# Head scores in three split products, sigmoids without reciprocals, and gate tile, rotation and root rows at other points, in a three-layer block kernel

## What is computed

```python
r = jax.nn.sigmoid(einsum(xb, wa) + ba)
i = jax.nn.sigmoid(einsum(xb, wx) + bx)
log_a = (LRU_C * r) * jax.nn.log_sigmoid(lam)
a = jnp.exp(log_a)
b = jnp.sqrt(-jnp.expm1(2.0 * log_a)) * (i * xc)      # h_t = a_t h_(t-1) + b_t
```

## Time and profile before

| | |
|---|---|
| median of 3 runs | 3032.59 us |
| the profiled execution's own time | 3033.25 us |
| its span, first to last instruction | 3031.2 us |
| TensorE busy (matmul) | 2968.0 us, 98% |
| VectorE, ScalarE, GpSimd busy | 53%, 43%, 45% |
| TensorE waiting for other work, all waits over 0.1 us | about 53 us |

### The profile page before, as it was taken

One profiled execution on the slowest core, in us unless ns is written; L12 is line 12 of the kernel. 1 busy time (PEld: TensorE's weight loads), 2 busy tenths in 40 slices (PEclk: granted clock), 3 DMA queues, 4 the chain that ended last, 5 costly groups with the idle time before them and its releaser, 6 DMA issues. The chain is left out here.

```text
span 3031.2 us, 48608 instructions
## 1 busy us (share of the span) xinstructions
PE 2968.0 (98%) x17338; PEld 2407.8 (79%) x17338; DVE 1616.7 (53%) x2411; ACT 1304.1 (43%) x2552; POOL 1351.8 (45%) x1022
## 2 busy tenths in 40 slices
PE   8999999999999999999999999999999999999998
PEld 6888888877777788878888877788888888777886
DVE  5377666655657306653556575551435565755412
ACT  6545444354556334453333334453533333344532
POOL 4444444443433356454444433344644444433444
PEclk9999999999999999999999999999999999999999
DMA  6322222222222334333322222243343222222433
GB/s 240 107 86 108 83 83 82 72 84 83 81 77 78 131 119 153 104 118 136 118 91 87 91 84 70 77 147 102 121 149 118 91 86 92 84 70 74 149 101 107
DMA packets 79010, 313.30 MB, mean 103 GB/s; under 512 B 7440, under 2 KB 11920, under 8 KB 51472
## 3 DMA queue, kind: packets, MB, share of 16 engines
q1 hardware_dynamic: 54832, 266.62, 26.1%
q10 hardware_dynamic: 24032, 44.76, 4.2%
HBM read 293.01 MB, written 18.35 MB: 103 GB/s over the span
## 5 line engine op out<-in xcount | busy, mean ns | idle before, releaser
L340 POOL TENSOR_TENSOR w_low<-w_raw,w_high 128x512 fp32r<-128x512 f32 x844 | 1136.1, 1351 | 1525.2 <-ACT w_high L851 1502.5
L405 PE MATMUL z<-u_high,w_high 128*128 128x512 f32 x3216 | 1277.4, 397 | 15.3 <-DVE work L1491 14.6
L406 PE MATMUL z<-u_low,w_high 128*128 128x512 f32 x3216 | 1257.9, 391 | 0.0
L851 ACT ACTIVATE w_high<-w_raw 128x512 fp32r<-128x512 f32 x832 | 520.0, 629 | 1112.6 <-PE z L409 1075.9
L409 PE MATMUL z<-u_high,w_low 128*128 128x512 f32 x3216 | 862.3, 390 | 0.0
L405 PEld LDWEIGHTS z<-u_high,w_high 128*128 128x128 f32 x3216 | 605.8, 188 | 165.2 <-issue 32.4
L409 PEld LDWEIGHTS z<-u_high,w_low 128*128 128x128 f32 x3216 | 605.0, 188 | 127.7
L406 PEld LDWEIGHTS z<-u_low,w_high 128*128 128x128 f32 x3216 | 606.3, 189 | 119.7
L1867 DVE TENSOR_TENSOR work<-work 128x512 f32<-128x512 f32 x78 | 90.9, 1165 | 277.5 <-ACT work L1140 264.8
L1491 DVE TENSOR_TENSOR work<-z,work 128x512 f32<-128x512 f32 x110 | 76.1, 692 | 181.9 <-PE z L409 145.3
L363 POOL TENSOR_TENSOR pass_weights<-w_raw,pass_weights 128x512 fp32r<-128x512 f32 x96 | 134.4, 1424 | 62.3 <-ACT pass_weights L1053 61.8
(11 more groups left out here) (341 smaller groups left out, 3698.3 us busy)
## 6 DMA issues: line engine op xcount, KB each, us to landing
w_raw<-in_wt SPq DMA_DIRECT2D x213, 1024.0 KB, 4.9
w_raw<-in_wt SPq DMA_DIRECT2D x144, 256.0 KB, 3.0
out_hT<-work ACTq DMA_DIRECT2D x10, 1024.0 KB, 5.8
work<-out_hT ACTq DMA_DIRECT2D x8, 1024.0 KB, 10.3
work<-in_xT SPq DMA_DIRECT2D x4, 1024.0 KB, 16.5
e_scratch<-work ACTq DMA_DIRECT2D x1, 4096.0 KB, 16.7
work<-in_xT ACTq DMA_DIRECT2D x4, 1024.0 KB, 10.9
mixed<-e_scratch ACTq DMA_DIRECT2D x4, 1024.0 KB, 9.2
```

The source lines that it names most:

```text
L340: pool.tensor_tensor(WL[:, 4 * q:4 * q + 4, :], RAW[:, t.odd, 512 * q:512 * q + 512].rearrange("p (k c) -> p k c", k=4), WH[:, 4 * q:4 * q ...
L405: pe.matmul(bank[:], WH[:, k, :], UH[:, k, :], start=(k == 0), stop=False)
L406: pe.matmul(bank[:], WH[:, k, :], UL[:, k, :], start=False, stop=False)
L851: act.activation(WH[:, 4 * q:4 * q + 4, :], RAW[:, n.odd, 512 * q:512 * q + 512].rearrange("p (k c) -> p k c", k=4), ACT.Copy).then_inc(se ...
```

## The change

The two heads' scores are formed from high and low parts of type fp32r, three products for each head, the heads taken in turn; `take_heads` makes the high parts by copies and the low parts by two more subtractions, on VectorE (`dif_scores` is changed as `att_scores` is, with its width w). The LRU's sigmoids are formed by exponential, logarithm, exponential on ScalarE; VectorE first reads both gates from PSUM, adds the bias and clips. The root row and the turn back stand one piece later, in the gated product's second half three pieces later. In the differential stages the first rotation is at point 7 in place of 6. In the first of them the gate tile is read at point 11 in place of 15, and the tile behind it right after the stage in place of point 3 of the next.

```diff
@@ -187 @@
+        QKH = nc.alloc_sbuf_tensor_at("heads_high", [P, 2, S], F32R, offset=work_at + 22 * S * 4)
+        QKL = sb("heads_low", [P, 2, S], F32R)
@@ -573 tensor engine, scores @@
+            def head_scores(n, hd, a, w):
+
+                o = slice(64 * hd, 64 * hd + 64)
+                q, k = ((QKH, QKH), (QKH, QKL), (QKL, QKH))[n]
+                return pe.matmul(SC[hd][:, 0:w], q[o, 0, a * P:(a + 1) * P], k[o, 1, 0:w], start=(n == 0), stop=(n == 2))
+
             def att_scores(j, a):
 
-                for hd in range(2):
-                    u = 2 * a + hd
-                    pe.wait_ge(sem("sm_done"), PRIMED + j * 8 + max(u - 1, 0))
-                    o = 64 * hd
-                    pe.matmul(SC[hd][:], row(QT)[o:o + 64, a * P:(a + 1) * P], row(KTR)[o:o + 64, :],
-                              start=True, stop=True).then_inc(sem("s_done"), 1)
+                for n in range(3):
+                    for hd in range(2):
+                        if n == 0:
+                            pe.wait_ge(sem("sm_done"), PRIMED + j * 8 + max(2 * a + hd - 1, 0))
+                        mm = head_scores(n, hd, a, S)
+                        if n == 2:
+                            mm.then_inc(sem("s_done"), 1)
...
@@ -770 tensor engine, norm_points @@
                 if pg:
-                    return {6: lambda: root_row(n),
-                            7: lambda: turn_back(n, (sem("pg_prod"), 14 + 2 * h), h, (0, 12), BACK_PG[h])}
-                return {3: lambda: root_row(n),
-                        4: lambda: turn_back(n, (sem("z_free"), t - T_HGG + (5 if h else 2)), h, (12,), BACK)}
+                    return {7 + 2 * h: lambda: root_row(n),
+                            8 + 2 * h: lambda: turn_back(n, (sem("pg_prod"), 14 + 2 * h), h, (0, 12), BACK_PG[h])}
+                return {4: lambda: root_row(n),
+                        5: lambda: turn_back(n, (sem("z_free"), t - T_HGG + (5 if h else 2)), h, (12,), BACK)}
@@ -947 ScalarE, ret_work @@
                 if p == 9:
-                    if cl is not None:
-                        act.wait_ge(sem("cl_ready"), cl)
+                    act.wait_ge(sem("gate_read"), PRIMED + j * 2 + 2)
                     for g in range(2):
-                        act.wait_ge(sem("gate_done"), j * 2 + g + 1)
-                        act.wait_ge(sem("scan_done"), PRIMED + j)
-                        act.activation(row(LR + g), SC[g][:], ACT.Exp, bias=SM[:, 32 + 6 * g + b:33 + 6 * g + b],
-                                       scale=-1.0).then_inc(sem("gate_read"), 1)
+                        sigmoid(LR + g, "r_ready")
                 if p == 10:
-                    act.wait_ge(sem("r_ready"), j + 1)
+                    act.drain()
@@ -1529 VectorE, take_heads @@
                 v.drain()
-                v.tensor_copy(row(QT), row(QN))
-                v.tensor_copy(row(KTR), row(KN)).then_inc(sem(done), 1)
+                for n, x in ((0, QN), (1, KN)):
+                    v.tensor_copy(QKH[:, n, :], row(x))
+                v.drain()
+                for n, x in ((0, QN), (1, KN)):
+                    i = v.tensor_tensor(QKL[:, n, :], row(x), QKH[:, n, :].bitcast(F32), ALU.subtract)
+                i.then_inc(sem(done), 1)
@@ -1688 VectorE, lru_work @@
                 if p == 9:
 
-                    v.wait_ge(sem("gate_read"), PRIMED + j * 2 + 2)
-                    v.tensor_scalar(view(LR, 0, [[1, 2 * S]]), view(LR, 0, [[1, 2 * S]]), 1.0, None, ALU.add)
-                    v.drain()
-                    v.reciprocal(R_, R_).then_inc(sem("r_ready"), 1)
-                    v.reciprocal(I_, I_)
+                    for g in range(2):
+                        v.wait_ge(sem("gate_done"), j * 2 + g + 1)
+                        v.tensor_scalar(row(LR + g), SC[g][:], SM[:, 32 + 6 * g + b:33 + 6 * g + b], GATE_MIN, ALU.subtract, ALU.max
+                                        ).then_inc(sem("gate_read"), 1)
                 if p == 10:
+                    v.wait_ge(sem("r_ready"), j * 2 + 2)
@@ -1789 VectorE, step @@
+                    if p == gate_taken_at:
+                        rstd_mul(t.plus(gate_tile_at), row(RW))
+                        bounded()
                     if work is not None:
...
-                            gate_tile(t.plus(gate_tile_at), gate[0], MIX[:, gate[1], :])
+                            if gate_taken_at is None:
+                                rstd_mul(t.plus(gate_tile_at), row(RW))
+                                bounded()
+                            gate_product(gate[0], MIX[:, gate[1], :])
@@ -2160 VectorE, the layer's order @@
-                dif = dict(rot=(CTD, STD, 32), scales=scd, take="dqt_ready", ends=(6, 10), gate_tile_at=2)
+                dif = dict(rot=(CTD, STD, 32), scales=scd, take="dqt_ready", ends=(7, 10), gate_tile_at=2)
                 step(Tile(T_L2 + R_DIF, (PER_LAYER, l)), gate=(gl + 6, 6), work="ret", j=l * RET_HEADS + RET_HEADS - 1, m=5,
-                     **{**dif, "ends": (3, 7)})
+                     **{**dif, "ends": (3, 7), "gate_taken_at": 11})
+                rstd_mul(Tile(T_L2 + R_DIF + 3, (PER_LAYER, l)), row(RW))
+                bounded()
                 step(Tile(T_L2 + R_DIF + 4, (PER_LAYER, l)), gate=(gl + 8, 7), work="dif", j=l * DIF_HEADS, m=6,
-                     between={3: lambda: lru_gate(Tile(T_L2 + R_DIF + 3, (PER_LAYER, l)), gl + 7, 0)}, **dif)
+                     between={3: lambda: lru_product(gl + 7, 0)}, **dif)
```

More of the change, by code:

```diff
@@ L659, in dif_scores @@
             def dif_scores(j, a):
[L661 to L666, removed]
+                w = (a + 1) * P
+                for n in range(3):
+                    for hd in range(2):
+                        if n == 0:
+                            pe.wait_ge(sem("dsm_done"), PRIMED + j * 8 + max(2 * a + hd - 1, 0))
+                        mm = head_scores(n, hd, a, w)
+                        if n == 2:
+                            mm.then_inc(sem("ds_done"), 1)
             def dif_values(j, a):
@@ L1508, in gate_tile, with gate_product @@
                 bounded()
+                gate_product(n, dst)
+            def gate_product(n, dst):
                 v.wait_ge(sem("gexp"), n + 1)
@@ L1774, in step @@
             def step(t, rot=None, scales=None, gate=None, hg=None, work=None, j=None, lru=None, take=None, ret=None, fin=None, open_gate=False, between={},
-                     ends=(3, 7, 11), gate_tile_at=3, **kw):
+                     ends=(3, 7, 11), gate_tile_at=3, gate_taken_at=None, **kw):
                 for p in range(16):
@@ L1828, in lru_gate, with lru_product @@
             def lru_gate(t, n, b):
-                gate_tile(t, n, row(RW))
+                rstd_mul(t, row(RW))
+                bounded()
+                lru_product(n, b)
+            def lru_product(n, b):
+                gate_product(n, row(RW))
                 v.tensor_tensor(MIX[:, 10 + b, :], MIX[:, 10 + b, :], row(RW), ALU.mult).then_inc(sem("lru_done"), 1)
```

## The result

| | before | after |
|---|---|---|
| median of the runs beside each other, us | 3033.68 (3032.46 to 3035.77, 4 runs) | 3016.84 (3015.69 to 3018.32, 4 runs) |
| profiled execution, us (its span) | 3033.25 (3031.2) | 3018.32 (3016.3) |

The ratio is 0.9945, 95% interval 0.9930 to 0.9961. The change gains 16.8 us, where 28 were forecast: the direction and the range held, the size did not. So 11 to 13 us are missing.

What follows compares the result with a forecast made beforehand. The prediction took TensorE, busy 98% of the span, as the bound, with its waits and the low clock behind them. Its terms, -18.9 - 5.4 - 6.1 + 8.4 - 5.9 = -27.9, gave 3005.3 us from 3033.25; range 2996 to 3022.

Steps and rivals of the forecast that it cites:

- Term 1: First differential stages: gate tile read at point 11 removes 14.6 us of wait and its low clock; -18.9 us.
- the residual wait: First differential stages: TensorE's remaining wait for the head copies, charged 0.5 us for both layers, 4 as the bad end.
- The sigmoids cost TensorE nothing: All 12 stages: ScalarE's sigmoids delay weight splits some 2 us, covered by slack; about 6 us less VectorE work per stage.
- Term 2: Root rows: moving them later by pieces of 1.36 us cuts TensorE's waits for the roots; -5.4 us.
- The wait of 2.99 us goes with three pieces: Second root row, at 1353.28: three pieces (4.1 us) remove TensorE's wait and 1.7 us of low clock; net -4.0.
- Term 3: Later differential stages: rotation at point 7 removes four waits for `dif_out` at point 8; -6.1 us.
- Term 4: Head copies in six differential stages: no slack, so subtractions with a drain add 1.4 us each; +8.4 us.
- Term 5: Scores by three fp32r products: groups shorter in attention (-5.0) and differential stages (-2.6), less copy costs; -5.9 us.
- A: Score groups: each weight load waits for the product before it, 1.06 us at width 512; time 3016; chance 0.12.
- B: Score groups: heads don't run side by side, 1.56 us at width 512; 3038.8 us, or about 3065; chance 0.10.
- C: First differential stages: VectorE late for another reason, TensorE waits 3 to 5 us per layer; 3013 to 3017; chance 0.10.
- D: Head copies: GpSimd holds each pair of subtractions for one operation, +12 us, time 3017; chance 0.08.

Runs made afterwards that it cites:

- roots_alone: The kernel before with only the root rows moved (points 7 and 9 for 6 and 6, 4 for 3): 3028.47 us, ratio 0.9988.
- heads_at_12: The changed kernel with heads of the differential stages, except each layer's first, taken at point 12 in place of 13: 3000.14 us, ratio 0.9885.
- scores_alone: The kernel before with only the scores changed, heads as high and low parts, three products per score: 3048.12 us, ratio 1.0048.
- dif_f32: The changed kernel with only the differential stages' scores back to plain float32 products from float32 head copies: 3003.61 us, ratio 0.9896.
- reciprocals_back: The changed kernel with the recurrence's sigmoids by reciprocals on VectorE again: 3014.32 us, ratio 0.9934.
- tile_alone: The kernel before with only the early gate tile read (point 11, next stage's tile ahead of that stage): 3016.69 us, ratio 0.9948.
- sigmoids_alone: The kernel before with only the sigmoids changed, from reciprocals on VectorE to ScalarE: 3034.21 us, ratio 1.0005.

## Why the prediction was right in sign and too large in size

The profiled runs differ by 14.9 us, where the sum gave 27.9. The difference of the start of the same operations in the two traces gives each term its size.

**Term 1, forecast -18.9: right in mechanism, 2.7 too large.** Before the first differential stage of layer 0 the changed kernel is 5.54 us ahead (the first quarter behind the passes starts at 1387.48, before at 1393.02), and at the quarter behind the first differential scores 13.95 (1804.31, before 1818.26): 8.4 us. In the second layer it is 11.38 ahead (2216.64, 2228.02) and then 19.21 (2633.10, 2652.31): 7.8, so 16.2 together. The step that failed is the residual wait, 0.5 for both layers; it was 1.65 and 1.28. The copies were to be ready at 1807.3 in the time of before; TensorE wanted them at 1807.7. VectorE's relief of 3.2 us came at the sigmoids and was lost again behind them, on operations that now meet GpSimd's: 0.4 us is left of it by the copies in the first layer and 0.8 in the second (waits of 2.06 us with reciprocals). The clock is 1.00 behind both waits, so the 4.8 us of clock came as forecast.

**The sigmoids cost TensorE nothing: right, but only as far as that sentence goes.** Their use was priced as VectorE's sum of busy time (6 us less in a stage). The chain through them is what counts.

**Term 2, forecast -5.4: measured -3.6, and 0.5 in region 2 (the closing whose root row waited 1.07 us before) that was not forecast.** A step of the sum failed. The next pass starts when its low parts are ready, whatever TensorE gained before. The forecast has that at 1367.3, which is 4.0 us before 1371.26 for both roots together, and then adds 1.4 for the first root again. It came at 1367.64 in `roots_alone`. "The wait of 2.99 us goes with three pieces" failed as well, for two reasons: the three pieces were counted from an arrival that the first root's gain brings forward (2.7 us later and not 4.1), and VectorE was taken to have the root ready when it had before, but it had it 1.5 us later. Of the 1.74 us of wait that is left, the first leaves 0.25 and the second adds the rest.

**Term 3, forecast -6.1: measured -5.8.** Right.

**Term 4, forecast +8.4: the waits were +8.2 (6 x 1.37), and with the low clock behind four of them +14.9.** The failed sentence is "Waits of 1.4 to 1.5 us left the clock alone in this trace". It was true of four waits of 1.52 to 1.53 us; behind four of six waits of 1.55 us it isn't. This is the largest error, 6.7 us. The place of the copies was also taken as given; `heads_at_12` shows 2.6 us of idle time of VectorE one point earlier.

**Term 5, forecast -5.9: the groups are right (0.17 at width 512; 0.31 for a differential head), and attention's share is short by the clock.** Attention brought 2.1 us up to 1295 in place of 3.3. The start of the kernel, up to the first quarter at 36 us, took 0.3 us longer in the changed kernel and 1.0 in `heads_at_12`. Counted from there attention brought 2.4 us in the changed kernel, with 1.7 us more lost to low clock than before, and 3.7 in `heads_at_12` and 3.6 in `scores_alone`, with as much low clock as before. So the forecast 3.3 is reached where the clock stays up. The rows below show the place: inside the values of the first pair TensorE has a wait put down to issue, of 1.41 us before and 2.23 after, and it ends at the same time although TensorE was there earlier.

```profile
649.01 0.32 PE L604 MATMUL v_bank<-work,values_spread 32*64 32x128 f32 x2 [2.23 <-issue]
```

```profile
649.03 0.32 PE L595 MATMUL turned<-work,values_spread 32*64 32x128 f32 x1 [1.41 <-issue]
```

The first fence is of the kernel after, the second of before. Behind it the clock is 0.72 in the kernel after (648 to 654), 1.7 us. What holds TensorE there was not tried and stays open. The seven kernels with three products in attention wait 2.2 to 2.4 us there, the six with float32 scores 1.4 to 1.7, and low clock stands behind five of the seven and one of the six. That the longer wait brings the clock down is an argument from these counts and not shown.

**The sum anew:** -16.2 - 3.6 - 0.5 - 5.8 + 14.9 - 2.1 - 2.5 (eight heads by 0.31) = -15.8. From the last root row, which the change doesn't touch, to the end of the span it is 1.0 us longer in this run than before (14.4 against 13.4), with more low clock: -14.8, where -14.9 was measured.

**The rivals.** A and B are refuted by the score groups: 0.89 us, where A needed 1.06 and B 1.56. The second and the third product start 0.23 us apart (698.59 and 698.82), as in a quarter (the first and the second 0.34), so a load does run under the product before it although both use the same rows of the array. Of the rule in the Trainium skill, TensorE: Matmul & The Clock Gate, "The mechanism", the second half, the background buffer, fits this; the rows don't name the buffer. C was right in part: VectorE was late for a reason that it gives (operations behind GpSimd's), by 1.3 to 1.7 us and not by 3 to 5. D is refuted: 30 of the 32 subtractions take 0.7 us and two take 1.8. The time of 3016.84 lies where A, C and D put theirs, but none of them is what happened; that the time lies where they put it is luck. The largest part of the miss is a term that none of them has, the low clock behind the six waits.

## What to carry to other kernels

Work added to an engine that is half idle isn't free where it stands last in front of the engine that bounds the kernel. Look in the timeline for that engine's idle time just before, and put the new work there: the same copies and subtractions, one point earlier, made this change worth 35 us and not 17. When several waits of one chain are moved, count each arrival anew from the one before it. And price a faster operation by the chain that goes through it: the sigmoids saved 3.2 us at their own place and 0.4 us at the end of the chain, and gave nothing until something was put in the time that VectorE waits for them. When an operation is moved, look also at what a second engine does beside it: the same VectorE operations took 5.1 or 9.3 us as they met GpSimd's.

## What was not expected of the hardware

Behind a wait of 1.55 us of an otherwise busy TensorE the granted clock can stand at its lower level (1.2 GHz), with 1.7 us lost, and it need not. Where `dif_f32` and `heads_at_12` take the waits away, the low clock is gone too. Of the waits of 1.55 to 1.66 us in the later differential stages, 9 of 20 had low clock behind them: 4 of 6 in the changed kernel, 5 of 9 in `scores_alone`, none of 5 in `reciprocals_back`. None of the 15 waits of 1.52 and 1.53 us in the kernel before, `tile_alone`, `roots_alone` and `sigmoids_alone` had any, nor had the six of 1.28 to 2.06 us for the heads' low parts in the first differential stages, nor one of 2.71 us in `sigmoids_alone`; of two of 1.90 and 1.91 us the shorter had it. So the length alone doesn't decide it, and what does stays open.
